# One 448-column product for both parts of the activations in the second expert layers, in two passes over the output features

## The reference, cut to what matters

```python
def peer_ffn(x, w_peer_q, peer_subkeys, peer_u, peer_v):
    ...                                   # top-16 of 128x128 experts per head, 8 heads
    experts = i1 * N_KEYS + i2            # N_KEYS = 128, so 16384 experts
    gates = jax.nn.softmax(best_s, axis=-1).astype(x.dtype)
    ...
    def chunk(args):
        xc, ec, gc = args
        u = peer_u[ec]
        act = jax.nn.gelu(jnp.einsum('tkd,td->tk', u, xc))
        return jnp.einsum('tk,tkd->td', gc * act, peer_v[ec])
```

## Time and profile before

| what | value |
|---|---|
| median of three runs | 3657.38 us |
| the profiled execution: time / span | 3656.89 / 3655.1 us |
| mean granted TensorE clock | 0.985 |
| TensorE busy | 3550.3 us (97%) |
| VectorE busy | 2298.7 us (63%) |
| ScalarE busy | 1572.5 us (43%) |
| GpSimd busy | 1485.2 us (41%) |
| products of line 1216 | 4096 with `unit_hi`, 2048 with `unit_lo` |
| first and last of them | 2469.0 and 3522.9 us |

### The profile page before, as it was taken

The page is one execution under the profiler, slowest core; times in us unless marked ns, Lnnn a source line. Parts: engine busy times, 40 slices in busy tenths (PEclk is TensorE's granted clock), DMA queues, the critical chain, the costliest instruction groups (busy, mean ns, idle before and its releaser), DMA issues.

```text
span 3655.1 us, 71614 instructions
## 1 busy us (share of the span) xinstructions
PE 3550.3 (97%) x30184; PEld 3428.9 (94%) x30184; DVE 2298.7 (63%) x3426; ACT 1572.5 (43%) x2015; POOL 1485.2 (41%) x671
## 2 busy tenths in 40 slices
PE   7999998999999999999999999999999999999998
PEld 3799897979998989999999999999999999999998
DVE  6586466784635557463214688786777666677755
ACT  7513433334344454464444434444444444444443
POOL 0247591008274858708898950001113000111136
PEclk8999999999999999999999999999999999999999
DMA  8456761855653535545555455557886555788843
GB/s 347 190 220 258 271 232 70 316 215 205 233 217 133 185 128 179 191 174 185 184 196 195 175 196 197 185 183 286 299 299 253 198 184 184 266 297 292 294 150 127
DMA packets 118123, 784.58 MB, mean 215 GB/s; under 512 B 13488, under 2 KB 13616, under 8 KB 31920
## 3 DMA queue, kind: packets, MB, share of 16 engines
q1 hardware_dynamic: 97056, 703.65, 51.1%
q0 software_dynamic: 18832, 67.94, 6.2%
q10 hardware_dynamic: 2016, 9.87, 0.7%
HBM read 778.49 MB, written 2.10 MB: 214 GB/s over the span
## 4 chain that ended last, share of the span: by engine, by line
PE 85%; DVE 7%; POOL 2%; DMA 2%; ACT 2%; issue 2%; SPq 0%; DVEq 0%; ACTq 0%; POOLq 0%
PE bank L622 54%; PE bank L1216 19%; DMA ring<-in_w 2%; POOL unit_lo L556 2%; PE bank L676 2%; PE bank L792 1%; PE bank L653 1%; ACT unit_hi L1265 1%; PE bank L1152 1%; DVE ada_acc L1788 1%; DVE unit_lo L1871 1%; PE bank L591 1%; PE bank L721 1%; PE bank L767 0%; PE bank L998 0%
## 5 line engine op out<-in xcount | busy, mean ns | idle before, releaser
L1265 ACT ACTIVATE unit_hi<-ring 128x1024 fp32r<-128x1024 f32 x1204 | 1240.3, 1056 | 1152.9 <-PE bank L622 431.1
L556 POOL TENSOR_TENSOR unit_lo<-ring,unit_hi 128x1024 fp32r<-128x1024 f32 x522 | 1334.3, 2578 | 973.8 <-ACT unit_hi L1265 972.8
L622 PE MATMUL bank<-xl_hi,unit_hi 128*128 128x256 f32 (+1 forms) x4688 | 1312.9, 280 | 21.8 <-DVE unit_lo L1871 6.4
L622 PE MATMUL bank<-xl_lo,unit_hi 128*128 128x256 f32 (+1 forms) x4688 | 1299.4, 277 | 0.0
L622 PE MATMUL bank<-xl_hi,unit_lo 128*128 128x256 f32 (+1 forms) x4688 | 1299.1, 277 | 0.0
L622 PEld LDWEIGHTS bank<-xl_hi,unit_hi 128*128 128x128 f32 x4688 | 895.5, 191 | 28.2 <-issue 10.9
L622 PEld LDWEIGHTS bank<-xl_hi,unit_lo 128*128 128x128 f32 x4688 | 895.1, 191 | 0.0
L622 PEld LDWEIGHTS bank<-xl_lo,unit_hi 128*128 128x128 f32 x4688 | 894.4, 191 | 0.5
L1216 PE MATMUL bank<-w_r,unit_hi 128*128 128x224 f32 x4096 | 688.3, 275 | 0.1
L1216 PEld LDWEIGHTS bank<-w_r,unit_hi 128*128 128x128 f32 x4096 | 622.7, 192 | 0.3 <-issue 0.3
L1216 PE MATMUL bank<-w_r,unit_lo 128*128 128x224 f32 x2048 | 565.7, 276 | 0.0
(11 more groups left out here) (487 smaller groups left out, 5531.6 us busy)
## 6 DMA issues: line engine op xcount, KB each, us to landing
ring<-in_w SPq DMA_DIRECT2D x669, 1024.0 KB, 4.9
resid<-in_xT ACTq DMA_DIRECT2D x4, 512.0 KB, 6.2
tmp_ctx<-in_ctxT ACTq DMA_DIRECT2D x4, 512.0 KB, 9.0
sgu_rows<-in_sgr ACTq DMA_DIRECT2D x1, 2048.0 KB, 8.9
rnn_gates<-in_rgw ACTq DMA_DIRECT2D x1, 2048.0 KB, 10.4
out<-resid SPq DMA_DIRECT2D x4, 512.0 KB, 2.6
pick<-in_eu,expert_idx POOLq DMA_INDIRECT x64, 4.7
pick<-in_ev,expert_idx POOLq DMA_INDIRECT x64, 4.8
```

What stands on the lines that cost most here:

```text
L556: pool.tensor_tensor(lb[b][:], ring[slot][:, f * HALF:(f + 1) * HALF], hb[b][:].bitcast(F32), ALU.subtract).then_inc(lo_done, 1)
L622: mm = pe.matmul(bank[(s.t0 + tile[m]) % TILES][:, 0:cols], w[b][:, (i % 8) * P:(i % 8 + 1) * P], mv[x][:, k, 0:cols], start=(k == 0 and w ...
L1265: act.activation(hb[b][:], ring[slot][:, f * HALF:(f + 1) * HALF], ACT.Copy).then_inc(hi_done, 1)
```

## The change

A unit of `peer_v` is now two rows of 128 experts by half the output features (the layout of the weights on the host changes with it), and the 64 units of a round are two passes p = 0, 1 of 32 units, each over all 64 rows and over eight output tiles. Each output tile has a whole bank: columns 0 to 223 collect w_hi x_hi + w_lo x_hi, columns 256 to 479 collect w_hi x_lo. The product with w_hi takes both parts of the activations as 448 moving columns. Four `w_r` buffers, two of them over tiles that are no longer used. The last unit of each pass and the first of the second go bank by bank (`banks_in_turn`), and VectorE adds the banks to `h` as they fill (`acc_out`), two additions per bank. The `ev` gathers go by halves of the features, and `expert_sums` is done in two parts.

```diff
+        def two_parts(b):
+            return b[:].rearrange("p (x t) -> p x t", x=2)[:, :, 0:TM]
...
         wr = [zone(f"w_r{i}", 113 + 1.75 * i, [P, 2, TM], F32R) for i in range(2)]
+        wr.append(place("w_r2", [P, 2, TM], F32R, mrow_at))
+        wr.append(place("w_r3", [P, 2, TM], F32R, con_at + 4 * COFF["tri_u"]))
...
             def fetch(table, q, before=0):
                 k = before + q
+                f, j = (q // PJ, q % PJ) if before else (q % 2, q // 2)
...
-            def expert_sums():
-                pe.wait_ge(S("pick_used"), 2 * PICKS)
-                for c in range(KC):
-                    pe.matmul(bank[c // 2][:, c % 2 * T + TM:(c % 2 + 1) * T], vsum[:, c * P:(c + 1) * P], owner[:],
+            def expert_sums(p):
+                pe.wait_ge(S("pick_used"), PICKS + PJ * (p + 1))
+                for c in range(8):
+                    pe.matmul(bank[c][:, TM:T], vsum[:, (8 * p + c) * P:(8 * p + c + 1) * P], owner[:],
                               start=False, stop=False, skip_group_check=True)
...
                 if r == 1:
-                    pe.wait_ge(S("acc_used"), 1)
+                    pe.wait_ge(S("acc_used"), 9)
...
-                def body(it, first, r=r, s=s, last_bank=last_bank):
...
+                def products(c, n, j, f, first, s=s):
+                    b = (2 * (s.n0 + j) + f) % NBUF
+                    x = wr[2 * (j % 2) + f]
+                    pe.matmul(two_parts(bank[c]), hb[b][:, c * P:(c + 1) * P], x[:], start=first, stop=False,
+                              skip_group_check=True)
+                    return pe.matmul(bank[c][:, 0:TM], lb[b][:, c * P:(c + 1) * P], x[:, 0, :], start=False, stop=False,
+                                     skip_group_check=True)
+                def halves(n, j, order, first, r=r):
+                    for f in range(2):
+                        pe.wait_ge(S("wr_ready"), 2 * r * I2 + 2 * n + f + 1)
+                        pe.wait_ge(lo_done, 2 * (s.n0 + n) + f + 1)
+                        for c in order[f]:
...
+                            mm = products(c, n, j, f, first and f == 0)
+                        mm.then_inc(half_done, 1)
+                def banks_in_turn(n, j, order, first, r=r):
+                    for f in range(2):
+                        pe.wait_ge(S("wr_ready"), 2 * r * I2 + 2 * n + f + 1)
+                        pe.wait_ge(lo_done, 2 * (s.n0 + n) + f + 1)
+                    for i, c in enumerate(order):
+                        if first:
+                            pe.wait_ge(S("acc_used"), 16 * r + i + 1)
+                        for f in range(2):
+                            mm = products(c, n, j, f, first and f == 0)
+                            if i == 7:
+                                mm.then_inc(half_done, 1)
+                        if not first and i < 7:
+                            mm.then_inc(S("acc_full"), 1)
+                for p in range(2):
+                    if p == 1:
+                        banks_in_turn(I2 // 2, 0, range(8), True)
+                        for j in range(1, 4):
+                            halves(I2 // 2 + j, j, plainly, False)
+                    with pe.Fori(8 * p + 1, 8 * p + 7) as it:
+                        for j in range(4):
+                            halves(j + it * 4, j, plainly, False)
+                    for j in range(3):
+                        halves(32 * p + 28 + j, j, plainly, False)
+                    if r == 1:
+                        expert_sums(p)
+                    banks_in_turn(32 * p + 31, 3, (1, 0, 2, 3, 4, 5, 6, 7) if p and not r else range(8), False)
...
             s = PLAN["pp"]
-            pe.wait_ge(S("rms_t"), NG + 1)
+            pe.wait_ge(S("acc_used"), 26)
...
+                        for f in range(2):
+                            act.activation(wr[2 * (j % 2) + f][:, 0, :], at_chunk(W, 2 * j + f - I2 * p + it * 8), ACT.Copy
+                                           ).then_inc(S("wr_hi"), 1)
...
+                def rests_of_rows(n, r=r):
+                    for q in (2 * n, 2 * n + 1):
+                        dve.wait_ge(S("wr_hi"), 2 * r * I2 + q + 1)
+                        dve.tensor_tensor(wr[q % 4][:, 1, :], at(W, q % I2), wr[q % 4][:, 0, :].bitcast(F32), ALU.subtract
+                                          ).then_inc(S("wr_ready"), 1)
...
+                def acc_out(p, r=r, s=s):
+                    for i, c in enumerate((1, 0, 2, 3, 4, 5, 6, 7) if p and not r else range(8)):
+                        x, cols = at(h, 8 * p + c), (TM, T)[r]
+                        if i < 7:
+                            dve.wait_ge(S("acc_full"), 14 * r + 7 * p + i + 1)
+                        else:
+                            dve.wait_ge(half_done, NBUF + 2 * (s.n0 + I2 // 2 * (p + 1)))
+                        go(dve.tensor_tensor(x[:, 0:cols], x[:, 0:cols], bank[c][:, 0:cols], ALU.add)); sync()
+                        dve.tensor_tensor(x[:, 0:TM], x[:, 0:TM], bank[c][:, T:T + TM], ALU.add).then_inc(S("acc_used"), 1)
                 for i in range(I2):
-                    if 1 <= i < I2 - 1:
-                        rest_of_row((i + 1) % 4, i + 1, i + 2)
+                    if i + 1 < I2:
+                        rests_of_rows(i + 1)
+                    if i == I2 // 2 - 1:
+                        acc_out(0)
                     if i + 2 < I2:
                         v_split(r, i + 2, 0)
                     for q in (PICKED_U, PICKED_V[1])[r][i]:
                         (expert_dot, expert_add)[r](q)
                     if i + 2 < I2:
                         v_split(r, i + 2, 1)
...
+                acc_out(1)
+                if r == 1:
+                    dve.wait_ge(S("acc_used"), 32)
+                    for g in range(NG):
+                        for c in range(GR * g, GR * g + GR):
                             go(dve.tensor_scalar(rt[:, c, :], h[:, c, :], V("ple_n", c), None, ALU.mult))
                         event("rms_t")
```

More of the change, by code:

```diff
@@ L726, in ple_sums @@
                 pe.wait_ge(S("rms_t"), NG + b)
+                if a == 0:
+                    pe.wait_ge(S("acc_used"), 29)
                 for k in range(GR * a, GR * b):
@@ L1210, in body @@
+                def halves(n, j, order, first, r=r):
[3 more added lines that the diff above has]
+                        for c in order[f]:
+                            if first and f == 0:
+                                if c == 7:
                                     settle(bank[7][:, 0:T], pairs[:, 32:32 + P, :].unsqueeze(1).to_broadcast([P, 2, P, 2]),
@@ L1211, in body @@
                                            pairs[:, 160:160 + I2, :].unsqueeze(1).to_broadcast([P, 2, I2, 2]), True)
-                                if first and j == 0 and cc == 2 * last_bank:
+                                if c == last_bank:
                                     pe.wait_ge(tile_free["A"], TILES + s.ta)
[L1214 to L1218, removed]
@@ new lines, in _ @@
+                plainly = (range(8), range(8))
+                halves(0, 0, ((4, 5, 6, 7, 1, 2, 3, 0), range(8)), True)
+                for j in range(1, 4):
+                    halves(j, j, plainly, False)
+                for p in range(2):
+                    if p == 1:
+                        banks_in_turn(I2 // 2, 0, range(8), True)
+                        for j in range(1, 4):
+                            halves(I2 // 2 + j, j, plainly, False)
[7 more added lines that the diff above has]
+                    banks_in_turn(32 * p + 31, 3, (1, 0, 2, 3, 4, 5, 6, 7) if p and not r else range(8), False)
@@ L2895, in _ @@
                         v_split(r, i + 2, 1)
-                s = PLAN[f"peer_v{r}"]
-                dve.wait_ge(half_done, NBUF + 2 * (s.n0 + s.npi * s.iters))
-                for b in ((1, 0, 2, 3, 4, 5, 6, 7) if r == 0 else range(8)):
-                    cols = (TM, T)[r]
-                    go(dve.tensor_tensor(h[:, 2 * b:2 * b + 2, 0:cols], h[:, 2 * b:2 * b + 2, 0:cols],
-                                         bank[b][:].rearrange("p (c t) -> p c t", c=2)[:, :, 0:cols], ALU.add))
-                    if r == 1 and b % 2:
-                        sync()
-                        for c in range(2 * b - 2, 2 * b + 2):
+                acc_out(1)
[3 more added lines that the diff above has]
+                        for c in range(GR * g, GR * g + GR):
                             go(dve.tensor_scalar(rt[:, c, :], h[:, c, :], V("ple_n", c), None, ALU.mult))
                         event("rms_t")
-                    if r == 0 and b in (1, 3, 7):
-                        event("acc_used")
             lo_rest("pg")
```

69 lines of the change are left out of this document (28 added, 41 removed).

## The result

The changed kernel takes 3614.8 us (median of 4 runs, 3610.81 to 3615.65) beside 3658.16 us for the kernel before (4 runs, 3655.84 to 3660.59): a ratio of 0.9887, 95% interval 0.987 to 0.9903. The forecast was 3611. The profiled execution took 3615.65 us (span 3613.8) against 3656.89 (span 3655.1): 41.2 us less, where the sum had 46.1 less.

A forecast was written before the change was run, and what follows sets the result against it. TensorE alone was taken to set the time in the second expert layers. The terms -47.9 + 4.3 + 1.5 - 0.8 - 0.7 - 2.5 = -46.1 took 3656.9 to 3611 us; the forecast's own range was 3598 to 3628.

The forecast's parts named there:

- The pair: Second expert layers, per weight block: three 224-column products (335.1 ns) become one of 448 and one of 224, 311.7 ns; -47.9 us.
- A: Rival on the products: the 448 streams at its columns' rate, short load partly hidden; pair 303.7 ns, 3594 us; chance 0.14.
- its second price: Rival on the products, second case: the short product at 101 ns, giving 3572 us in all.
- B: Rival in the second layers' units: VectorE becomes the bound, a unit at 5.2 us gives back 27, 3638 us; chance 0.10.
- C: Rival on the products: the 448 in two runs costs a full bank's 229 ns; pair 342 ns, 3673 us; chance 0.05.
- The turn: Between the two passes, TensorE waits behind VectorE's bank additions: stops 3.0 and 1.3 us, +4.3, plus +1.5 for the clock.
- The +1.5 for the clock: Behind the stops between the passes, a slower clock costs +1.5 us in all, bounds 0 and 6.
- End of r=0: Before the next first layer, additions run beside the last unit, so the 0.83 us stop goes: -0.8 us.
- Expert sums in two parts: Weak products in two stretches of half the length lose less to the half clock: -0.7 us, bounds -1.4 and +1.4.
- The tail: End of r = 1: the stop before "pp" goes, "pg" starts at 16.5 us; -2.5 us, bounds -8 and +3.

The follow-up runs named there:

- e3_turn: Changed kernel with the two copies for w_r of the second pass's second row moved ahead on VectorE; 3611.07 us, ratio 0.9891 to the kernel before.
- e2_three: Changed kernel with the wide product undone, two products of 224 columns in its place, all else kept; 3655.1 us, ratio 1.0005 to the kernel before.
- a_after: The changed kernel itself, unedited, run once more beside later kernels on another chip; 3615.2 us, ratio 0.9894 to the kernel before.
- e4_tail: Changed kernel with ScalarE's evictions for the last projection put ahead of the squares in the tail; 3613.83 us, ratio 0.9898 to the kernel before.

## Why the prediction was right, and where a size was off

**TensorE sets the time, and the pair is what pays: right.** The kernel with the passes and without the wide product is where the kernel before is.

**The pair, 311.7 ns forecast, 314.7 measured (saving 41.8 us, not 47.9): the term that was mis-sized.** The step was the straight line from 256 to 512 columns, 200 for the 448, with 111.7 behind it. By itself the 448 takes 202.2, 2 ns over that line, and the 224 its 111.7. Together they cost 1.5 ns more than alone (315.4 against 313.9). That makes 3.7 ns of 311.7, of which the kernel shows 3.0, on 2048 pairs 6.1 us; the other terms gave 1.2 of them back. In the kernel the short product shows 105 and the long one 210, though alone they take 112 and 202: the split by starts says little, and the pair is what to count.

**Rivals.** A is out: its pair of 303.7 put the 448 at 192 ns, and by itself it takes 202.2; its second price needed a short product of 101, below the 112 of the floor, and 128 columns in place of 224 take only 3 ns off the pair. The formula of the Trainium skill, "TensorE: Matmul & The Clock Gate", section "Back-to-back issue gap", is given there for an isolated product and has 189 ns for the 448 (an estimate by that page) and 215.8 for the 512. In streams where each product brings its own weight block they took 202.2 and 227.2, so it is not the price here. B is out: VectorE keeps 16% in the middle of the layer, and the unit follows the pair (16 x 314.7 = 5.035). C is out: the 448 in two runs of addresses takes 202.2, not the 227.2 of a full bank.

**The turn, +5.8 forecast (stops 4.3, clock 1.5), 5.0 measured (3.3 and 1.7).** Mechanism, order and releaser were right. The additions took 0.72 us a bank, not 0.75, and a longer unit gave VectorE a little more time. That much of this hangs on the place of two copies e3_turn shows: 3.5 us of it go, and the rest is mostly the 0.94 us stop a unit later. The +1.5 for the clock was a choice between two rows of the kernel before, so that it came within 0.2 us is partly luck: in e2_three a stop of 1.8 us cost no clock at all.

**End of r=0, -0.8: right.** There is no stop of 0.83 us before the next first layer. The layer between is 0.5 us longer, with one new stop of 0.2 for a low half of VectorE; this was not in the sum.

**Expert sums in two parts, -0.7 forecast, -1.4 measured.** Behind each half of the weak products the clock is 1.00. This was the bound, and the trace of before could not tell.

**The tail, -2.5 forecast, -2.4 measured, in part by luck.** Group 0 is done at 6.6 us and ScalarE's first "pp" copy starts at 8.6, both as worked out. "pg" starts at 17.6 and not at 16.5. The term left out that TensorE's new stop of 3.72 us would be followed by half clock: 5.8 us of it, in which the second "pp" unit runs. In a_after, the same kernel, the half clock behind the same stop ended after 3.3 us, and "pg" starts at 16.4. That did not matter: in both executions the last projection's long run begins 32.0 us behind the last product, where the kernel before has 33.9. So the change is worth -1.9 here. The other 0.5 us are two small products near the end of the kernel (line 767, line 755 before) that took 0.71 us in this execution and 1.24 in a_after and in the kernel before.

The rule of the Trainium skill ("SBUF — State Buffer", section "SBUF: two separate sides") on which the step leaned, that the pair of ports that VectorE and GpSimd share is an exclusive lock for a whole instruction, agrees with the trace: 4.67 against 1.14 us for the same four instructions, and 2.41 to 2.47 us for each of the four beside GpSimd's four in e4_tail. e4_tail shows that TensorE's stop does not set the tail. That VectorE's waits for GpSimd do is read from the rows; no run took GpSimd's work away.

The measured terms: -41.8 + 5.0 - 0.8 - 1.4 - 2.4 + 0.3 + 0.5 = -40.6, and the profiled executions differ by -41.2. The calls of `settle` that fell away are another -1.2. With every term taken from start to start the pair is 335.0 - 314.8 = 20.2 ns (-41.4 in all), the turns +5.3, the end of r=0 -1.0 and the sums -1.6; with the calls, the tail (-2.4) and the two stretches outside these layers (+0.3, +0.5) this adds up to -41.5.

## What to carry to other kernels

Price a product by two numbers of the trace: the floor, which is the time that a short product with a weight block of its own doesn't go below, and the slope of its columns. Interpolate only between widths that lie above the floor: here 112 ns, and 25 to 29 ns for each 64 columns above 256. Merging two products under one stationary block saves a floor and pays for its columns, so it should pay most where both are short: by the numbers here, as an estimate that no run tested, two products of 128 columns take 224 ns and one of 256 takes 120. When a loop is cut in two passes, look at what the engine that drains the banks has queued behind the drain. Here the stop was made by that queue, and moving two small copies ahead in it took off most of what the turn cost.

## What the runs showed of the hardware

- GpSimd's indirect DMA issue, after and then in the kernel with three products (instruction views of their line):

```profile
L523 POOL DMA_INDIRECT pick<-in_eu,expert_idx x64: 990/1867/1930, 2464.4 to 2782.8; - x64
```

```profile
L523 POOL DMA_INDIRECT pick<-in_eu,expert_idx x64: 932/936/1958, 2463.3 to 2799.2; - x64
```

  The median is 1.87 us against 0.94, with the same code. In the changed kernel's timeline one such issue stands behind the start of a subtraction on VectorE:

```profile
2561.89 1.23 DVE L2816 TENSOR_TENSOR unit_lo<-ring,unit_hi 128x1024 fp32r<-128x1024 f32 x1
2562.06 1.87 POOL L523 DMA_INDIRECT pick<-in_eu,expert_idx  x1 [3.16 <-DVE expert_dot L2828]
```

  It ends at 2563.93, 0.81 us behind the end of that subtraction (2563.12). All 61 issues of the changed kernel from 2475 to 2810 us start more than 0.04 us behind the start of a VectorE instruction that is still running, and each ends 0.81 us behind that instruction's end, within 0.01 us. In the kernel with three products 8 issues do, and end 0.81 us behind it too; the other 53 start with the VectorE instruction or beside none and take 0.94. So an issue waits for the VectorE instruction that it finds running. It cost nothing here.
- Products of 256 columns ran at 113.5 or 117.9 ns in the same code, by execution (3.1 us in the last projection), at a granted clock of 1.00 both times. The cause is open.
- A stop of 2.4 us was followed by seven pairs in 3.89 us, where full rate would be 2.20; stops of 1.8 us (e2_three) and 0.9 us by full rate. The same stop of 3.7 us was followed by 5.8 us at half clock in one execution of the changed kernel and 3.3 us in another.
- While GpSimd ran instructions one behind another, VectorE got one scaling done for each of them: about 2.4 us instead of 0.29 (e4_tail).
